# A macaron transformer layer: first feature tile by plain products, token sums on the vector engine, attention by pairs of heads

## The reference

```python
x = x + 0.5 * swiglu_ffn(rms_norm(x, g1), w_gate1, w_up1, w_down1)      # d_ff = 2816
P = rms_norm(x, g_mix) @ w_in       # attn q|k|v (512 each), hgrn q|f|i|g (512 each)
A = chunked_band_attention(rms_norm(q), rms_norm(k), v, rel_bias)       # 8 heads x 64
B = hgrn2(...)                      # 4 heads x 128, gated linear recurrence
x = x + concat(A, B) @ w_out
x = x + 0.5 * swiglu_ffn(rms_norm(x, g2), w_gate2, w_up2, w_down2)
```

## Time and profile before

| | |
|---|---|
| median of 3 runs | 2057.04 us (2053.04 to 2062.95) |
| the profiled execution | 2058.25 us |
| its span, first to last instruction | 2056.5 us |
| mean granted TensorE clock | 0.976 |
| TensorE busy | 1951.3 us, 95% |
| weight loads (beside the matmuls) | 1614.9 us, 79% |
| vector engine busy | 1169.6 us, 57% |
| ScalarE busy | 697.9 us, 34% |
| GpSimd busy | 477.9 us, 23% |
| DMA | 144 GB/s in the mean |

### The profile page before, as it was taken

How to read it: one execution, slowest core, us unless ns; L and a number is a source line. 1 busy time by engine, 2 the same in 40 slices (tenths; PEclk the granted TensorE clock), 3 DMA queues, 4 the chain that set the end, 5 groups by cost and what they waited for, 6 DMA issues and landing times.

```text
span 2056.5 us, 24576 instructions
## 1 busy us (share of the span) xinstructions
PE 1951.3 (95%) x9272; PEld 1614.9 (79%) x9272; DVE 1169.6 (57%) x1507; ACT 697.9 (34%) x1053; POOL 477.9 (23%) x375
## 2 busy tenths in 40 slices
PE   4599999999999999999998999986999999999999
PEld 3488888887888888888886777865888888878887
DVE  5667667665555630344454554348667667655564
ACT  6333333332333432112114554243233333323332
POOL 4433233242102100010134220015233242230120
PEclk8799999999999999999998999998999999999999
DMA  3344444446766343332244110111544444458663
GB/s 134 109 162 139 170 169 146 156 149 247 270 194 195 113 149 113 113 102 92 86 134 157 61 55 1 52 72 48 178 166 145 160 169 158 149 184 307 215 194 133
DMA packets 209004, 295.50 MB, mean 144 GB/s; under 512 B 14512, under 2 KB 104760, under 8 KB 208896
## 3 DMA queue, kind: packets, MB, share of 16 engines
q1 hardware_dynamic: 193184, 253.28, 36.2%
q0 software_dynamic: 7504, 26.03, 4.0%
q10 hardware_dynamic: 8208, 14.75, 1.9%
HBM read 205.37 MB, written 91.25 MB: 144 GB/s over the span
## 4 chain that ended last, share of the span: by engine, by line
PE 90%; DVE 5%; ACT 2%; DMA 1%; issue 1%; POOL 1%; SPq 1%; DVEq 0%; ACTq 0%; POOLq 0%
PE ps L629 26%; PE ps L631 26%; PE ps L630 26%; PE ps L865 3%; PE ps L903 2%; PE ps L784 2%; PE ps L886 2%; PE ps L663 1%; DVE xs L1339 1%; DVE xs L1314 0%; DVE hTlo L1328 0%; DVE wlo L1377 0%; DVE xs L1341 0%; DMA raw<-ffn_w_up 0%; DVE xs L1344 0%
## 5 line engine op out<-in xcount | busy, mean ns | idle before, releaser
L629 PE MATMUL ps<-hThi,whi 128*128 128x512 f32 x832 | 326.3, 392 | 21.5 <-DVE wlo L1377 15.8
L630 PE MATMUL ps<-hTlo,whi 128*128 128x512 f32 x832 | 325.3, 391 | 0.0
L631 PE MATMUL ps<-hThi,wlo 128*128 128x512 f32 x832 | 325.2, 391 | 0.0
L629 PE MATMUL ps<-whi 128*128 128x512 f32 x616 | 242.5, 394 | 9.2 <-DVE wlo L1425 9.2
L629 PE MATMUL ps<-hXhi,whi 128*128 128x512 f32 x528 | 209.7, 397 | 42.8 <-POOL hXlo L1736 26.4
L631 PE MATMUL ps<-whi,wlo 128*128 128x512 f32 x616 | 241.6, 392 | 0.0
L630 PE MATMUL ps<-wlo,whi 128*128 128x512 f32 x616 | 241.6, 392 | 0.0
L630 PE MATMUL ps<-hXlo,whi 128*128 128x512 f32 x528 | 208.8, 396 | 0.0
L631 PE MATMUL ps<-hXhi,wlo 128*128 128x512 f32 x528 | 208.6, 395 | 0.0
L1377 DVE TENSOR_TENSOR wlo<-raw,whi 128x512 fp32r<-128x512 f32 x176 | 148.4, 846 | 94.4 <-ACT whi L1048 94.4
L629 PEld LDWEIGHTS ps<-hThi,whi 128*128 128x128 f32 x832 | 157.3, 189 | 54.6 <-DVE wlo L1377 16.0
(11 more groups left out here) (176 smaller groups left out, 3174.8 us busy)
## 6 DMA issues: line engine op xcount, KB each, us to landing
hid_scratch<-hid SPq DMA_DIRECT2D x132, 256.0 KB, 3.0
raw<-ffn_w_gate SPq DMA_DIRECT2D x44, 512.0 KB, 3.7
raw<-ffn_w_up SPq DMA_DIRECT2D x44, 512.0 KB, 5.0
wdb<-ffn_w_down SPq DMA_DIRECT2D x44, 512.0 KB, 4.1
wd_scratch<-wdb SPq DMA_DIRECT2D x88, 256.0 KB, 4.5
raw<-hid_scratch SPq DMA_DIRECT2D x80, 256.0 KB, 2.7
rawx<-hid_scratch SPq DMA_DIRECT2D x74, 256.0 KB, 2.7
raw<-w_in SPq DMA_DIRECT2D x28, 512.0 KB, 5.0
```

Source lines behind the costliest of these rows:

```text
L629: pe.matmul(dst, ahi, bhi, start=first, stop=False, skip_group_check=onto)
L630: pe.matmul(dst, ahi, blo, start=False, stop=False, skip_group_check=onto)
L631: return pe.matmul(dst, alo, bhi, start=False, stop=last, skip_group_check=onto)
```

## The change

**1. Tile 0 of each feed-forward stage by eight plain products.** No weight sums: gate and up, each of two halves of the input features, each for two halves of the tokens (for the second token half T1 stands in place of its first 512 features, and the kept products (0,0) and (0,1) are added back). Tile 1's products that need no more than T1 are moved ahead of the others. Weights are numbered apart from products (`WEIGHTS`), since each of tile 0's four serves two products, and have eight places in turn.

**2. Token sums.** `t_sums` becomes `t1`, `t2` and `t34` (T3 and T4 in one instruction over 1024 columns), issued in three rounds over the four token blocks; their low parts are `t1_lo`, `t2_lo`, `t34_lo` on the vector engine, and GpSimd's `t_lo` goes.

**3. Norm weights of FFN1** are loaded by ScalarE's queue, as its first instruction, with a semaphore of their own.

**4. Attention by steps w of two units** (the same token tiles of both heads): their scores matmuls alternate, head 0's on rows 0 to 63 and head 1's on rows 64 to 127; their values matmuls alternate, each with its own 64 columns of `vin` and its own 64 partitions of one bank. `S`, `Pr` and `PT` have four places. One `keep_out` a step takes all 128 rows. q and k of the next pair are transposed in four halves through bank 7, the outputs too; squares, sums and scaling stand one to two units earlier. Copies to `PT` come two units after the exponential instead of one.

The core of the diff:

```diff
+PLAIN_WEIGHT = (0, 1, 2, 3, 2, 3, 0, 1)
+PLAIN_BANK = (0, 1, 0, 1, 2, 3, 2, 3)
+PLAIN_OPERAND = (0, 0, 2, 2, 6, 6, 4, 4)
-START = [(0, 0), (1, 0), (0, 2), (1, 2), (0, 1), (0, 3), (0, 4), (0, 5), (0, 6),
-         (1, 1), (1, 3), (1, 4), (1, 5), (1, 6)]
+START = [(0, 0), (0, 1), (1, 0), (0, 2), (0, 3), (1, 2), (0, 4), (0, 5), (0, 6), (0, 7),
+         (1, 4), (1, 1), (1, 3), (1, 5), (1, 6)]
-SQUARE_AT, SUM_AT, NORM_AT, TURN_QK_AT = (2, 5), (4, 7), (6, 9), (8, 10)
+SQUARE_AT, SUM_AT, NORM_AT = (1, 3), (3, 5), (5, 7)
+TURN_QK_AT = [(3, 1, 7), (4, 0, 8), (4, 1, 9), (5, 0, 10)]
+SLOTS = 4
...
             def gate_up(F, e, i):
-                if (e, i) == (0, 1):
-                    pe.wait_ge(t_ready, 12 * F + 11)
+                if (e, i) == (1, 1):
+                    pe.wait_ge(t2_ready, 4 * F + 4)
+                if (e, i) == (1, 3):
+                    pe.wait_ge(t34_ready, 4 * F + 4)
...
+            def scores(w):
+                p, _, parts = unit(2 * w)
+                if w:
+                    pe.wait_ge(unit_max, 2 * w)
...
+                            for hd in range(2):
+                                rows = slice(hd * DH, (hd + 1) * DH)
+                                last[hd] = pe.matmul(ps[:, b + c:b + c + m], qT[rows, p % 2, t * P:(t + 1) * P],
...
+            def values(w):
...
+                        for hd in range(2):
+                            rows = slice(hd * DH, (hd + 1) * DH)
+                            mm = pe.matmul(ps[rows, b:b + P], vin[:, p % 2, t - n + 1 + c, rows],
+                                           PT[:, (2 * w + hd) % SLOTS, c0 + c * P:c0 + (c + 1) * P],
...
+            for w in range(STEPS + 2):
+                if w < STEPS:
+                    scores(w)
+                if 1 <= w <= STEPS:
+                    turn(2 * w - 2)
+                halves(w, 0)
+                if w >= 2:
+                    values(w - 2)
+                if 1 <= w <= STEPS:
+                    turn(2 * w - 1)
+                halves(w, 1)
...
+            act.dma_start(gain[:, :], ffn1_norm_g[0:1, :].to_broadcast([P, D])).then_inc(gain1_loaded, 16)
...
+            def t34(F, j):
+                first = xs[:, j, :].rearrange("p (h c) -> p h c", h=2)
+                dve.wait_ge(t2_made, 4 * F + j + 1)
+                dve.tensor_tensor(first, xs[:, 4 + j, HALF:D].unsqueeze(1).to_broadcast([P, 2, HALF]), first,
+                                  ALU.subtract).then_inc(t34_made, 1)
...
             rms(R_FFN1)
-            for j in range(4):
-                t_lo(0, j)
```

More of the change, by code:

```diff
@@ L168, in by_scalar @@
     return v % 3 == 2
-def extra(v):
-    found = [("qk", v // NU + 1, w) for w in range(2)
-             if v < NV - NU and v % NU == TURN_QK_AT[w]]
-    found += [("out", p, g) for p in range(PAIRS) for g in range(2) if v == NU * p + TURN_OUT_AT[g]]
-    return found[0] if found else None
 def turn_bank(R, t):
@@ L323, in operand @@
         def operand(i, k):
[L325 to L328 removed]
+            if i in (S3, A22, S2):
+                return [a[:, {S3: 0, A22: 4, S2: 8}[i] + k, :] for a in (hXhi, hXlo)]
             kt, half = {0: (0, 0), 2: (4, 0), 4: (0, 1), 6: (4, 1)}[i]
@@ L665, in turn_tile, with plain @@
                 mm.then_inc(turned, 1)
+            def plain(F, i):
+                R = R_FFN2 if F else R_FFN1
+                w = weight_no(0, i)
+                pe.wait_ge(w_ready, NW * F + w + 1)
+                if i == 0:
+                    pe.wait_ge(hT_ready, TT * R + 4)
+                    pe.wait_ge(z_copied, TT + 6 if F else 1)
+                if i in (2, 3):
+                    pe.wait_ge(plain_kept, 2 * F + i - 1)
+                if i == 4:
+                    pe.wait_ge(hT_ready, TT * R + TT)
+                if i == 6:
+                    pe.wait_ge(t1_ready, 4 * F + 4)
+                for k in range(4):
+                    mm = three(bank(PLAIN_BANK[i]), [weight(a, w, F)[:, k * P:(k + 1) * P] for a in (whi, wlo)],
+                               operand(PLAIN_OPERAND[i], k), k == 0 and PLAIN_FIRST[i], k == 3, not PLAIN_FIRST[i])
+                mm.then_inc(prod_done, 1)
             def gate_up(F, e, i):
-                n = seq(e, i)
-                R = R_FFN2 if F else R_FFN1
-                pe.wait_ge(w_ready, SEQ * F + n + 1)
+                w = weight_no(e, i)
+                pe.wait_ge(w_ready, NW * F + w + 1)
                 if i == 0 and e >= 2:
@@ L916, in turn_out, with halves @@
                 mm.then_inc(out_turned, 1)
-            for v in range(NV + 3):
-                if v < NV:
-                    scores(v)
-                if 1 <= v <= NV:
-                    turn(v - 1)
-                if 2 <= v <= NV + 1:
-                    values(v - 2)
-                what = extra(v)
-                if v == NV + 2:
-                    turn_tile(R_CAT, 0)
-                    turn_tile(R_CAT, 1)
-                if what is not None:
-                    if v <= NV:
-                        wait_PT(pe, v - 1)
-                    if what[0] == "qk":
-                        turn_qk(what[1], what[2], 4)
-                    else:
-                        turn_out(what[1], what[2])
+            def halves(w, place):
+                p, step = w // OUT_STEPS, w % OUT_STEPS
+                if place == 0:
+                    for g in range(2):
+                        for q in range(PAIRS - 1 if g else PAIRS):
+                            if out_step(q, g) == w:
+                                turn_out(q, g)
+                if p + 1 < PAIRS:
+                    for n in range(4):
+                        if TURN_QK_AT[n][:2] == (step, place):
+                            turn_half(p + 1, n)
+            for w in range(STEPS + 2):
[9 more added lines that the diff above has]
+                halves(w, 1)
+            turn_tile(R_CAT, 0)
+            turn_tile(R_CAT, 1)
+            turn_out(PAIRS - 1, 1)
             for h in range(2):
@@ L1398, in after_product @@
-                if i == 5:
+                if i == (3 if e == 1 else 4) and e:
+                    up1(F, e)
+                if e and i == 5:
                     if t >= 2:
@@ L1671, in _ @@
                         norm_qk(v // NU + 1, NORM_AT.index(v % NU))
-                what = extra(v)
-                if what is not None and what[0] == "out":
-                    if what[1] == 0 and what[2] == 0:
-                        dve.wait_ge(ro_stored, 16 * HH)
-                    if v == NV + 2:
-                        hT_lo(R_CAT, 0)
-                    head_output(what[1], what[2])
+                for p in range(PAIRS):
+                    for g in range(2):
+                        if (p, g) != (PAIRS - 1, 1) and 2 * out_step(p, g) == v:
+                            if p == 0 and g == 0:
+                                dve.wait_ge(ro_stored, 16 * HH)
+                            head_output(p, g)
+            hT_lo(R_CAT, 0)
+            head_output(PAIRS - 1, 1)
             hT_lo(R_CAT, 1)
```

629 lines of the change are left out of this document (359 added, 270 removed).

## The result

| | before | after |
|---|---|---|
| median | 2057.51 us (2053.04 to 2062.95) | 1977.10 us (1975.67 to 1979.15) |
| ratio, 95% interval | | 0.9609 (0.9584 to 0.9634) |
| profiled execution | 2058.25 us | 1979.15 us |
| its span | 2056.5 us | 1977.6 us |

What follows compares the result with a forecast made beforehand. TensorE, 90% of the chain that ended last, was taken as the bound, so time goes only where it waits or its work shrinks. Gains of 27 + 21.5 + 30 = 78.5 us took 2058.25 to 1980, range 1967 to 2015.

Steps and rivals of the forecast that it cites:

- FFN1: First feature tiles of the first feed-forward stage: tile 2 starts at 78.1 instead of 105.14, 27 us gained.
- FFN2: First feature tiles of the second feed-forward stage: tile 2 at 1432.0 instead of 1453.66, 21.5 us gained, range 18 to 24.
- Attention: Attention stage, both heads on separate array halves: ends at 1241.7 instead of 1272, 30 us gained.
- Overlap: Attention, two units a step: scores 1.5 us and values 1.5, against 2.54 and 2.42 without overlap, 1.27 and 1.21 with full overlap.
- my walk: Attention's queues followed in order with assumed durations: stage ends at 1241.7, with ideal halves 1236, without overlap 1276.6, old order 1272.5.
- Waits: Attention: TensorE waits 3.4 us a pair of heads, 1.8 of them for late copies; a pair takes 31.8 instead of 40.25.
- First pair: Attention's first pair of heads, with both heads behind `ro_ready` and a load: 6 us shorter.
- rival (b): Attention: matmuls follow one another as before, the tighter order costs 4 us, 2014 us in all; chance 0.15.
- Rival (a): Attention: only row halves or only column halves overlap, 17 us gained instead of 30, 1993 in all; chance 0.17.
- (c): Attention: each change between array halves waits until the former matmul is through, 75 us in 24 steps, 2089 in all; chance 0.04.
- The other signs: New profile: no TensorE wait behind GpSimd, a 5 us `gu_u` wait in FFN1, half as many copies of `outT`.
- a danger: Attention: the clock might fall because TensorE rests a sixth of the time there, making the whole forecast wrong.

Runs made afterwards that it cites:

- roots_first: Changed kernel with GpSimd taking the inverse roots of q and k ahead of the bias masks: 1975.4 us, 0.9592 of before.
- both_serial: Changed kernel with head 1's scores behind a unit's transposes and values on all 128 columns, one head after the other: 2032.6 us, 0.9877 of before.
- roots_and_load: Changed kernel with inverse roots ahead of bias masks and the second pair's q and k loaded right behind the first pair's v: 1967.5 us, 0.9560 of before.
- masks_too: roots_and_load with the first pair's bias masks ahead of the load of its v: 1968.3 us, 0.9564 of before.

## Why the prediction was right

**Mechanism and sum.** All three terms came out: 27 against 27.1, 30 against 29.8, 21.5 against 20.6.

**FFN1** held in its steps too. The first product came at 22.40 (forecast 22.8), (1,0) at 32.90 (33.4), (1,3) at 67.77 (67.3), tile 2 at 78.01 (78.1). The vector engine had the split for (1,0) at 37.07 plus 0.69 and `gu_u` done at 67.67: 29.9 us for the chain that I had put at 29.8. It could be counted from the rows of before because its operations run back to back at 0.60 and 1.14 us. That it fits to 0.1 us is luck: I counted 25 operations of 512 columns where the trace has 24, and one of them (a weight split at 65.32) took 1.67 us instead of 0.60, beside GpSimd, which makes sums of the down weights from 65.21 on. I had assumed that GpSimd would be quiet here, and at this point it is not.

**FFN2.** The first product came 110.4 us behind the output projection's start instead of 122.0, 11.6 gained against 9.8. Product (1,3) started 147.9 us behind it, 0.5 earlier than forecast, but it had waited 2.25 us, not 1.5, and behind the wait the clock fell, which I had left up: its matmuls of line 636 start 1.42 and 1.28 us apart instead of 0.68 (rows in the last section). That costs 1.5 us (the product takes 4.27), and the term ends 0.9 short.

**Attention** came out right by errors that cancel:
- *Overlap.* 1.5 us for each kind was too cautious: 1.28 and 1.25, the ideal halves, which by my walk were worth 5.5 us more than forecast. TensorE's own work in a pair is 6 x 3.91 us and six half-transposes of 0.53, 26.6 us, not 28.4. My reason against values, that small matmuls are paced by something else than streaming, does not hold across the halves: each head's ten still take 1.25 us, but the two heads' run side by side, 1.25/20 = 0.062 an instruction.
- *Waits.* 3.4 us a pair were forecast; the pair from 1148.88 to 1180.38 takes 31.5, so 4.9 are waits (2.51 of them at 1168.88, which roots_first made shorter), and in the pair before, which has the same waits but takes 33.1, the clock fell behind one of them (its scores at 1136.86 are shown at 2.50 us instead of 1.35).
- *First pair.* 46.6 us before, 37.9 now, 8.7 less, but its first scores start 2.7 us later behind the recurrence than before, since they wait for what both heads need: 6.0, for 6 forecast.

So the mechanism, two halves at once, is shown, but the 30 us are right in part by luck: more overlap and more waits than forecast, nearly equal in size.

**The price of rival (b)** was wrong by the most. My walk over the new order without overlap ended 4 us later than over the old; both_serial is 21 us slower than before in attention, 2032.6 in all, and not 2014. A pair takes 44.8 us there, against 40.25 before, though TensorE's own work comes to 40.1 in it by an estimate from the rows above (six steps of 3.91 + 2.24, six half-transposes of 0.53): so some 4.7 us of waits a pair stay when the work grows, which the walk had taken to be covered by it. It is not quite that case (one copy more a step, scores on either side of transposes), but the order needs the overlap. Had it failed, the time would have been outside my range. Rival (a) is out, since both kinds overlap, and so is (c): twenty values matmuls that alternate between the halves take 1.25 us, so nothing drains between them.

**The other signs.** No wait behind GpSimd, a `gu_u` wait of 6.5 us for the 5 to 6 forecast, half as many copies of `outT`: as said. The clock did fall in attention, in its first pair (mean granted clock 0.81), in the second (0.95) and in the last (0.95), which I had named as a danger; the second and the last pair lost about 1.6 us each by it (33.1 and 37.6 us, where the third pair takes 31.5 and the last of roots_and_load 36.0, both without a fall).

## What to carry to other kernels

Matmuls that use half of the array cost nothing here if the other half's stand beside them in the queue; alternate them one by one, and don't part them by work on the whole array. Work taken from GpSimd is cheaper for the vector engine than its count says, as long as GpSimd then rests: count the old operations at their undisturbed length, and look what GpSimd turns to next. A change of loop order is a test of overlap only if the profile shows that the work was really parted. A queue that feeds nobody urgently, here GpSimd's, still decides by its order: put what the next engine waits for ahead of what is only due later.

## What the runs showed of the hardware

- TensorE let a matmul on one half of the array start while three on the other half that stood ahead of it had not started, in scores (row halves, four and six instructions a head) as in values (column halves, ten a head). With four a head no time was lost by their order (1.29 us), with six 0.74 us, with ten 0.70.
- Going from whole-array transposes to a group on half of the array costs 0.08 us (0.69 instead of 0.61), not the 0.28 us for which a matmul is shown.
- GpSimd and the vector engine both slow down beside one another: 0.68 to 1.78 us for a sum of 512 columns, and on GpSimd 2.35 to 3.04 us for a difference of 1024. It hits the operations that read both operands from SBUF: `gu_u`, which has one from PSUM, took its 0.68 us at 66.99 although GpSimd was at work (from 66.60 to 68.19).
- Behind a wait of 2.25 us TensorE's clock fell from its upper to its lower level (2.4 to 1.2 GHz): of the changed kernel's product (1,3) in FFN2, the first matmul starts at 1365.88 (above) and the next ones 1.42 and 1.28 us apart; from 1369.47 to 1370.15 it is 0.68 again.

```profile
1367.30 0.63 PE L636 MATMUL ps<-hXhi,whi 128*128 128x512 f32 x1
1368.58 0.60 PE L636 MATMUL ps<-hXhi,whi 128*128 128x512 f32 x1
```

- Such a fall does not follow from the length of the wait alone. Behind the 2.51 us at 1168.88 the clock stayed up: the next scores are shown at 1.35 us, while those behind the 2.44 us at 1135.76 are shown at 2.50. And in the last pair of masks_too and of roots_and_load TensorE waits 0.97 and 1.01 us at the same two places; behind them the values of masks_too, at 1198.21, take 2.40 us and those of roots_and_load, at 1202.20, 1.31.
